# A two-layer decoder trunk: a fourth pair of FFN weight tiles, one-tile norm sums, and convolution taps in later slots

## The reference

```
h = rmsnorm(x);  proj = h @ w_in            # 1024 -> q, k, v (512 each), conv value and gate (512 each)
q, k = rope(rmsnorm(q)), rope(rmsnorm(k))   # 8 heads of 64
attn = dilated_attention(q, k, v)           # three dilated windows, mixed by their softmax sums
u = causal_dwconv(value * sigmoid(gate))    # 31 taps per channel
u = silu(layernorm(u))
x = x + concat(attn, u) @ w_out
h = rmsnorm(x);  up = causal_dwconv(h @ w_up)      # 1024 -> 2 * 2816, 3 taps
x = x + (silu(gate) * val) @ w_down                # 2816 -> 1024
```

## Time and profile before

| | |
|---|---|
| time, median of 3 runs | 2455.23 us (2452.87 to 2455.89) |
| time of the profiled execution | 2451.28 us |
| its span in the profile | 2449.5 us |
| PE busy | 2412.9 us, 99% |
| DVE busy | 1569.2 us, 64% |
| ACT busy | 791.4 us, 32% |
| POOL busy | 150.3 us, 6% |

### The profile page before, as it was taken

How to read it: one execution, slowest core, us unless ns; L and a number is a source line. 1 busy time by engine, 2 the same in 40 slices (tenths; PEclk the granted TensorE clock), 3 DMA queues, 4 the chain that set the end, 5 groups by cost and what they waited for, 6 DMA issues and landing times.

```text
span 2449.5 us, 30576 instructions
## 1 busy us (share of the span) xinstructions
PE 2412.9 (99%) x11672; PEld 2011.9 (82%) x11672; DVE 1569.2 (64%) x1507; ACT 791.4 (32%) x1050; POOL 150.3 (6%) x57
## 2 busy tenths in 40 slices
PE   8999999999999999999999999999999999999998
PEld 6788898888888888888777888988888888888887
DVE  5998886656555555555639887866555555555554
ACT  4222665432222222222332226744322222222220
POOL 0121001100000000000102210011000000000000
PEclk9999999999999999999999999999999999999999
DMA  4333540111111111111112344301111111111111
GB/s 146 90 86 106 128 104 10 52 44 46 50 51 51 51 43 51 44 50 50 36 44 69 86 137 113 79 18 47 57 43 52 35 51 51 51 51 43 51 43 77
DMA packets 45522, 152.37 MB, mean 62 GB/s; under 512 B 7297, under 2 KB 8961, under 8 KB 45441
## 3 DMA queue, kind: packets, MB, share of 16 engines
q1 hardware_dynamic: 44576, 148.88, 21.0%
q10 hardware_dynamic: 864, 2.36, 0.2%
HBM read 129.97 MB, written 21.23 MB: 62 GB/s over the span
## 4 chain that ended last, share of the span: by engine, by line
PE 93%; DVE 4%; ACT 1%; issue 1%; DMA 0%; DVEq 0%; SPq 0%; ACTq 0%; POOLq 0%
PE mm L409 61%; PE aux L409 20%; PE aux L558 5%; PE mm L522 3%; PE aux L542 3%; DVE y L1073 2%; PE aux L436 1%; DVE w_lo L1004 1%; PE aux L445 0%; DVE x_lo L1016 0%; DMA x<-xT 0%; PE aux L503 0%; ACT w_hi L698 0%; DVE x L1010 0%; DVE o L1122 0%
## 5 line engine op out<-in xcount | busy, mean ns | idle before, releaser
L409 PE MATMUL mm<-x_hi,w_hi 128*128 128x512 f32 x2304 | 721.9, 395 | 19.5 <-DVE x_lo L1016 11.6
L409 PE MATMUL mm<-x_hi,w_lo 128*128 128x512 f32 x2304 | 716.2, 392 | 0.0
L409 PE MATMUL mm<-x_lo,w_hi 128*128 128x512 f32 x2304 | 715.1, 392 | 0.0
L409 PEld LDWEIGHTS mm<-x_hi,w_hi 128*128 128x128 f32 x2304 | 431.9, 189 | 113.5 <-issue 11.6
L409 PEld LDWEIGHTS mm<-x_lo,w_hi 128*128 128x128 f32 x2304 | 434.8, 189 | 94.6
L409 PEld LDWEIGHTS mm<-x_hi,w_lo 128*128 128x128 f32 x2304 | 434.7, 189 | 93.0
L698 ACT ACTIVATE w_hi<-w_raw 128x1024 fp32r<-128x1024 f32 x188 | 197.0, 1058 | 751.8 <-PE mm L409 556.2
L1073 DVE SCALAR_TENSOR_TENSOR y<-u_pad,cpar,y 128x1024 f32<-128x1024 f32 x240 | 314.2, 1336 | 3.7 <-ACT y L753 2.6
L1010 DVE TENSOR_TENSOR x<-x,aux 128x1024 f32<-128x1024 f32 x176 | 214.6, 1219 | 126.5 <-PE aux L409 116.9
L1004 DVE TENSOR_TENSOR w_lo<-w_raw,w_hi 128x1024 fp32r<-128x1024 f32 x188 | 233.1, 1248 | 52.1 <-ACT w_hi L698 46.2
L1022 DVE TENSOR_TENSOR uv<-mm,rinv 128x1024 f32<-128x1024 f32 x44 | 53.9, 1225 | 224.8 <-PE mm L409 224.6
(11 more groups left out here) (161 smaller groups left out, 2354.9 us busy)
## 6 DMA issues: line engine op xcount, KB each, us to landing
w_raw<-weights SPq DMA_DIRECT2D x188, 512.0 KB, 3.6
qk_scratch<-m SPq DMA_DIRECT2D x64, 128.0 KB, 2.1
qk_scratch<-o SPq DMA_DIRECT2D x64, 128.0 KB, 2.1
x_hi<-qk_scratch SPq DMA_DIRECT2D x32, 256.0 KB, 6.4
q_first<-qk_scratch SPq DMA_DIRECT2D x8, 512.0 KB, 4.7
k_hh_first<-qk_scratch SPq DMA_DIRECT2D x16, 256.0 KB, 5.8
k_ll_first<-qk_scratch SPq DMA_DIRECT2D x16, 256.0 KB, 6.3
x_hi<-qk_scratch SPq DMA_DIRECT2D x8, 512.0 KB, 4.8
```

Of the source, the lines that this page charges most:

```text
L409: last = pe.matmul(acc[:, cols], a, b[:, cols], start=start and n == 0, stop=stop and n == 2)
```

## The change

- `w_hi` and `w_lo` get a fourth entry, the tiles `q_first` and `k_hh_first`, which attention uses and the FFN does not. FFN unit f takes slot (f + 2) % 4. `hi` and `lo` are issued four units ahead instead of three; at the start of each group of the loop two are issued, and none at its end. ACT's wait for `down_full` at the end of the loop's body stays.
- At the layer boundary ACT copies units 0 and 1 at once, and DVE splits unit 0 before its first addition and unit 1 after it.
- DVE adds `squares[0]` into `squares[4]` with one more addition per norm, and waits for `sq_added` there instead of PE; PE sums one tile. In the FFN's first units the sums stand one block later, behind (1, 5).
- Slot `own` has 4 taps instead of 8; `gate` of pass 1 has 8 instead of 5; a new slot `norm`, between the gate's read and the q/k norm, has 4 in pass 2 and none in the others; `v1` has 7 instead of 5. The attention steps get 43 taps instead of 48.

```
-    slots = {"own": (0,) * 8}
+    slots = {"own": (0,) * 4}
...
-        slots[i, "value"], slots[i, "gate"] = (tiles * 2)[:4], (tiles * 3)[:5]
+        slots[i, "value"], slots[i, "gate"] = (tiles * 2)[:4], (tiles * 4)[:8 if i == 1 else 5]
+        slots[i, "norm"] = (tiles * 2)[:4 if i == 2 else 0]
...
-    slots["v0"], slots["v1"], slots["v2"] = (CT - 1, CT - 2) * 2, ((CT - 1, CT - 2) * 3)[:5], (0, 1, 0, 1)
+    slots["v0"], slots["v1"], slots["v2"] = (CT - 1, CT - 2) * 2, ((CT - 1, CT - 2) * 4)[:7], (0, 1, 0, 1)
...
+        w_hi.append(q_first)
+        w_lo.append(k_hh_first)
...
+        def ffn_slot(f):
+            return (f + 2) % 4
...  # norm_sums on PE
-                    pe.wait_ge(sq_added, at(l, 2 * SQ_ADDS, (norm + 1) * SQ_ADDS))
                     pe.wait_ge(sq_added2, at(l, 2, norm + 1))
-                    sums((squares[0], squares[KT // 2]), ones[:, 0:1], 1, s0)
+                    sums((squares[KT // 2],), ones[:, 0:1], 1, s0)
...  # first_up_units on PE
-                    order = [(n, k) for n in range(2) for k in range(4)] + [(0, 4), (0, 5), (1, 4), "sums", (1, 5)]
+                    order = [(n, k) for n in range(2) for k in range(4)] + [(0, 4), (0, 5), (1, 4), (1, 5), "sums"]
...  # ACT, start of a layer
                 hi(0, 0)
+                if l:
+                    hi(1, 1)
                 for t in range(KT):
                     if l == 0 and t == 1:
                         hi(1, 1)
-                    if l and t == KT - 2:
-                        act.wait_ge(down_full, l * DOWN)
-                        hi(1, 1)
...  # ACT, FFN loop
-                        hi((f - 1) % 3, U_FFN + f + 2, 12, j)
+                        hi(ffn_slot(f + 2), U_FFN + f + 2, 12, j)
+                        hi(ffn_slot(f + 3), U_FFN + f + 3, 12, j)
                         for n in range(4):
                             up(g, n, j)
                         act.wait_ge(down_full, at(l, DOWN, g * KT, 2 * KT, j))
-                        hi((f + 4) % 3, U_FFN + f + 7, 12, j)
...  # DVE, add_square
-                    add = dve.tensor_tensor(squares[KT // 2], squares[KT // 2], squares[t], ALU.add)
+                    dve.tensor_tensor(squares[KT // 2], squares[KT // 2], squares[t], ALU.add)
+                    dve.drain()
                     if t == KT - 1:
-                        add.then_inc(sq_added2, 1)
-                    dve.drain()
+                        dve.wait_ge(sq_added, at(l, 2 * SQ_ADDS, (norm + 1) * SQ_ADDS))
+                        dve.tensor_tensor(squares[KT // 2], squares[KT // 2], squares[0], ALU.add).then_inc(sq_added2, 1)
+                        dve.drain()
...  # DVE, start of layer 1
+                    lo(0, 0)
                     for m in range(KT):
                         add_to_x(m, aux[m % 2], down_full, down_read, (GROUPS - 1) * KT + m, DOWN, layer=l - 1)
                         if m == 0:
-                            lo(0, 0)
+                            lo(1, 1)
                         else:
                             first_splits(m - 1)
-                        if m == KT - 1:
-                            lo(1, 1)
...  # DVE, in-projection
                     conv_gate(i + 1, 5 + 4 * i)
+                    taps(i, "norm")
                     qk_norm(i)
```

More of the change, by code:

```diff
@@ L626, in up @@
                 def up(g, n, j=0, **more):
-                    unit(up_unit(g, n) % 3, n % 2, U_FFN + up_unit(g, n), M_UP + 4 * g + n, 12, 8, j, **more)
+                    unit(ffn_slot(up_unit(g, n)), n % 2, U_FFN + up_unit(g, n), M_UP + 4 * g + n, 12, 8, j, **more)
                 def down(g, j=0):
@@ L638, in down @@
                         for k in range(2):
-                            s = (f + k) % 3
+                            s = ffn_slot(f + k)
                             last = split_product(aux[m % 2], (w_hi[s][:, cols], w_lo[s][:, cols]),
@@ L661, in first_up_units @@
                         cols = slice(k * P, (k + 1) * P)
-                        last = split_product(mm[n], (w_hi[n][:, cols], w_lo[n][:, cols]),
+                        last = split_product(mm[n], (w_hi[ffn_slot(n)][:, cols], w_lo[ffn_slot(n)][:, cols]),
                                              (x_hi[:, k, :], x_lo[:, k, :]), k == 0, k == KT - 1)
@@ L899, in _ @@
                 unit_done(M_OUT + 13)
-                hi(0, U_FFN)
+                hi(ffn_slot(0), U_FFN)
                 for t in range(4, 6):
@@ L907, in _ @@
                     if t == 5:
-                        hi(1, U_FFN + 1)
+                        hi(ffn_slot(1), U_FFN + 1)
                 for t in range(6, KT):
                     square(1, t, squares2)
-                hi(2, U_FFN + 2)
+                hi(ffn_slot(2), U_FFN + 2)
                 small_mean(TB, S_NORM2, D_MODEL)
@@ L914, in _, with up @@
                 read_rinv(B_NORM2)
-                def up(g, n, j=0, ahead=True):
+                def up(g, n, j=0, ahead=4):
                     f, q, t = up_unit(g, n), 4 * g + n, 2 * g + n // 2
@@ L920, in up @@
                     if ahead:
-                        hi(f % 3, U_FFN + f + 3, 12, j)
+                        hi(ffn_slot(f + ahead), U_FFN + f + ahead, 12, j)
                     u, c = ((ug, cg), (uv, cv))[n % 2]
@@ L937, in _ @@
                 for n in range(4):
-                    up(0, n, ahead=n < 3)
+                    up(0, n, ahead=3 if n < 3 else 0)
                 with act.Fori(0, GROUPS // 2) as j:
@@ L1277, in _ @@
                 out_add(6, [1])
-                lo(0, U_FFN)
+                lo(ffn_slot(0), U_FFN)
                 add_square(5, squares2, 1)
@@ L1283, in _ @@
                     if t == 5:
-                        lo(1, U_FFN + 1)
+                        lo(ffn_slot(1), U_FFN + 1)
                 for t in range(6, KT):
                     add_square(t, squares2, 1)
-                lo(2, U_FFN + 2)
+                lo(ffn_slot(2), U_FFN + 2)
                 dve.memset(ug[:, 0:FFN_TAPS - 1], 0.0)
@@ L1292, in _, with up @@
                 dve.wait_ge(statb_read, at(l, STAT_B, B_NORM2 + 2))
-                def up(g, n, j=0, ahead=True, between=()):
+                def up(g, n, j=0, ahead=4, between=()):
                     f, q, t = up_unit(g, n), 4 * g + n, 2 * g + n // 2
@@ L1306, in up @@
                     if ahead:
-                        lo(f % 3, U_FFN + f + 3, 12, j)
+                        lo(ffn_slot(f + ahead), U_FFN + f + ahead, 12, j)
                     dve.drain()
@@ L1335, in _ @@
                         f = up_unit(g, 0)
-                        lo((f - 1) % 3, U_FFN + f + 2, 12, j)
+                        lo(ffn_slot(f + 2), U_FFN + f + 2, 12, j)
+                        lo(ffn_slot(f + 3), U_FFN + f + 3, 12, j)
                         for n in range(3):
@@ L1341, in _ @@
                             down(g - 1, m, j)()
-                        lo((f + 4) % 3, U_FFN + f + 7, 12, j)
                 if l == DEPTH - 1:
```

## The result

| | before | after |
|---|---|---|
| time, median (range) | 2455.31 us (2451.12 to 2460.05, 6 runs) | 2438.57 us (2437.97 to 2440.82, 6 runs) |
| profiled execution, span | 2451.28, 2449.5 | 2438.82, 2437.0 |
| mean granted clock | 0.996 | 0.999 |

The changed kernel is faster: ratio 0.9935, 95% interval 0.9922 to 0.9947, 16.7 us between the medians. I had said 25.3 us and 2430, with 2438.0 as the upper end. The direction was right; a third of the gain is missing, and the time lies above the range.

The account below looks back on a forecast made before the run. PE, busy 99% of the span, was taken as the bound; -9.2 + 1.8 - 2.1 - 1.7 - 6.0 - 2.9 - 4.6 - 0.6 = -25.3 us took the median from 2455.2 to 2429.9, said as 2430; range 2424.5 to 2438.

Parts of the forecast that it names:

- part 1: First pass: four taps less bring unit 8's lo forward, ending PE's idle 2.8 and slow 1.8 us; -9.2 over two layers.
- Unit 16: Pass 2: the moved taps make DVE's lo of this unit late, so PE waits 0.9 us a layer; +1.8.
- parts 1 and 2: Taps leaving the first pass, -9.2 us, and their landing in later slots, +1.8.
- part 3: One-tile sums at four norms: -2.1 and -1.7 us at the first norms, -6.0 at the second norms.
- part 4's ends: Fourth weight pair: -2.9 and -4.6 us at the two layers' last down stages, -0.6 at the layer boundary.
- that rival: The clock keeps falling beside the shorter norm sums, 1.7 us a fall, three to five falls: 2435 to 2438; 12%.
- Within the loop each group has the same 6 `hi`, 6 `lo` and 6 loads as before, only ordered otherwise; 0.: FFN loop: the fourth weight pair and its new order were taken to change no time, 0 us.
- Nothing is to be had there: FFN loop's down stage: 96 matmuls in 22.15 us without a pause, 0.231 us each, taken as leaving no gain.
- Nothing in these rows prices that at more than 0.4 a layer; I take 0.: Attention: POOL's third addition now falls among the steps; priced at 0, at most 0.4 us a layer.
- The bounds of part 2: Possible extra cost of moved taps, 0.4 (POOL's third addition) and 0.5 us (unit 19's lo) a layer; used in the upper end.
- the median should be 2455.2 - 25.3: Whole kernel: the profiled execution lay 4.0 us below the median, so the saving was taken from the median: 2429.9.
- The term of 2.1 for layer 0's first norm: Layer 0's first norm: 1.75 us less sums and 0.4 us of the slow stretch back before unit 2; -2.1.

Follow-up runs that it names:

- b_norm: The kernel before with the one-tile norm sums alone: 2443.2 us, ratio 0.9957.
- a_edge: The kernel after with slot 2's weight tiles at bytes 115840 to 124032 of a partition and slot 3's at 124032 to 132224: 2430.4 us, ratio 0.9909.
- b_gap: The kernel before with three gaps in SBUF (160, 32 and 448 bytes) and no other edit: 2437.8 us, ratio 0.9931.
- a_gap_hold: The kernel after with three gaps (160, 32, 448 bytes) and one tap held back to the last attention step: 2410.4 us, ratio 0.9822.
- b_taps_hold: The kernel before with the new schedule of taps, the last tap held back to the last attention step: 2447.0 us, ratio 0.9965.
- a_gap: The kernel after with three gaps (160, 32, 448 bytes), so x, h and all weight tiles start at 128 modulo 512: 2416.0 us, ratio 0.9845.
- a_pad: The kernel after with a gap of 32 bytes ahead of q_first, so all tiles allocated behind it lie 32 bytes higher: 2434.0 us, ratio 0.9916.
- b_pad: The kernel before with the gap of 32 bytes alone: 2453.3 us, ratio 0.9998.

## Why the prediction was wrong, step by step

**Right.** Unit 8 starts without a wait in both layers, and the slow stretch behind it is gone: part 1. Unit 16 is late by 0.9 us in both layers (PE idle 0.77, the rest in the first matmul), as forecast; DVE's idle time of 4.26 fell to 3.44 (3.4 forecast), that of 5.06 is gone. With the last tap held, parts 1 and 2 are worth 7.2 (7.4 in the sum); part 3 is worth 9.6 (9.8); part 4's ends 9.8 (8.1, the only one of these off by over 1 us). PE's wait behind the second norms is 0.3 us in two, 0.8 forecast. In the kernel after the clock fell behind no norm's sums: that rival did not come here, though it did once each in b_norm and a_edge. So the parts clean give 7.2 + 9.6 + 9.8 = 26.6 against 25.3; all at once, from b_gap to a_gap_hold, they give 27.4.

**Wrong, the larger step: "Within the loop each group has the same 6 `hi`, 6 `lo` and 6 loads as before, only ordered otherwise; 0."** It counts the instructions of ACT, DVE and SP, and takes a matmul's duration as fixed. Other slots mean other pairs of tiles for PE, and a pair of tiles has its own rate: 7.6 us in the trace. "Nothing is to be had there", of the down stage, was wrong too. The sign stood in the earlier trace rows: 22.15 / 96 is 0.231 us a matmul, and 11.00 / 48 is 0.229 although it holds a slow first matmul behind the sums (without it, 32.67 / 144 = 0.227). I wrote both down and asked nothing. A matmul takes 0.227 at best, and the loop held 16 us.

**Wrong, the second step: "Nothing in these rows prices that at more than 0.4 a layer; I take 0."** POOL's third addition among the steps cost 1.7 and 3.2 us in the trace (in layer 1 with the clock's fall), and 4.9 to 6.4 in medians with it and without it (five pairs of kernels). I had a price for POOL beside DVE, a tap of 3.42 instead of 1.28, and did not ask which of DVE's instructions would stand beside the addition, nor that PE waits for what follows it.

**The upper end was added up wrong.** The bounds of part 2 are "0.4 and 0.5 a layer", 0.9 a layer and so 1.8 in two; the range took 0.9. With 1.8 its end is 2430 + 6.8 + 1.8 = 2438.6, which is where the time lies. It would have been luck: the end stood on four falls of the clock behind the sums, and none came.

**The account closes in the traces.** 25.3 less 7.6 (the loop) and 4.9 (1.7 + 3.2 in attention) is 12.8; the two profiled executions differ by 12.5. The medians differ by 16.7, since the profiled execution of the kernel before was a lucky one: it kept the full clock at layer 0's last down stage and behind the sums of layer 1's first norm, and others do not. The timed executions of the kernel before beside the experiments show how much that is: the 19 with a mean granted clock of 0.996, the profile's, have a median of 2452.7 us, the 8 with 0.993 one of 2456.8. The same two stretches of b_taps_hold, which has the old weights and norms (columns as in the earlier trace rows):

```profile
1200.70:1204.70 4.00, 3.50 (x10) 2.77 (x11) 0.45 (x1) 0.00 (x0) 0.00 (x0) 0.68 0.39 131
1247.70:1251.10 3.40, 3.40 (x9) 2.72 (x10) 0.00 (x0) 0.24 (x2) 1.64 (x1) 0.50 0.00 0
```

Against the kernel before they cost it 1.5 and 3.0 us. Of the kernels run on the base of the kernel before, the clock fell at the first place in all five that still have its pause, and at the second in five of the six that still have its 32 rows. The kernel after has neither the pause nor the rows. My step "the median should be 2455.2 - 25.3" carried the 4.0 us between that execution and the median over unchanged; by these stretches they were mostly falls that the change takes away, though the timed executions have no traces to show where theirs were. Without this error in my favour the miss would have been larger.

The term of 2.1 for layer 0's first norm looks missed: unit 2 began only 1.4 us earlier, and in the 13 profiles with one-tile sums between 1.9 earlier and 0.3 later than in the kernel before. But the scatter lies ahead of the sums. The chain's first matmuls, kernel before and kernel after:

```profile
14.49 17.05 PE mm L409 x72
...
14.44 17.85 PE mm L416 x72
```

The same 72 take up to 19.39 (a_gap_hold); why they differ was not looked into. From the start of the sums to unit 2 it is 41.12 - 31.54 = 9.6 us before and 39.70 - 32.29 = 7.4 after, and 7.4 to 8.2 in all 13 profiles: 2.2 us, as the sum had it.

## What to carry to other kernels

A clock of 1.00 behind a pause in one execution does not say that the pause is free. Where PE is 99% busy, divide every unbroken stage by its count: 0.227 and 0.231 us a matmul are different things, and a change of buffers can be a change of rate. For matmuls of this form, try giving all tiles that meet in them the same start modulo 256 bytes. When the last member of a chain of work is moved, find what it starts on another engine (here POOL's addition), where that will fall, and what PE waits for just behind it.

## What was not expected of the hardware

- With 128x128 float32 weights and 512 moving columns, matmuls follow each other at 226.7 ns when all weights and moving operands start at the same byte modulo 256 (a_gap, b_gap), and at 232.4 to 234.4 at six of the seven other multiples of 32 (64 is between, 228.9 to 229.2 in most places). Nothing is waited for, the weight loads read 188 ns in both a_gap and the kernel after, and the clock is 1.00.
- Why, was not shown. That it depends on the two addresses and not on the order is shown by gaps alone. Two things are open. In a_pad a unit of `x` with slot 2, distance 64, took 10.99 us as the third of a group and 11.20 as the first of the next. In b_pad `h` with slot 2, distance 0, took 231.0 ns a matmul. So something beside the distance has a say.
- A theory of place gave one of three times within its range and the other two within 1.3 us of it, and was false. It fell on units, not on times: one stage in two that stayed at 22.40.
